# Expert weights in half-megabyte units: 48 units and 24 slots per pair of experts in place of 24 and 12

## The reference, cut to what matters

```python
aff = jax.nn.softmax((h @ w_router).astype(jnp.float32), axis=-1)
gates, idx = lax.top_k(aff.transpose(0, 2, 1), cap)          # cap = 64
xe = h[bidx, idx]
hg = jnp.einsum('becd,edf->becf', xe, w_gate)
hu = jnp.einsum('becd,edf->becf', xe, w_up)
y = jnp.einsum('becf,efd->becd', jax.nn.silu(hg) * hu, w_down)
y = y * gates[..., None].astype(y.dtype)
return jnp.zeros_like(h).at[bidx, idx].add(y)
```

## Time and profile before

| | |
|---|---|
| median of 3 runs | 2509.53 us (2507.8 to 2515.42) |
| the profiled execution, its own time | 2508.35 us |
| span of the trace, first to last instruction | 2506.8 us |
| TensorE busy, share of the span | 90% |
| granted TensorE clock, mean | 0.947 |
| weights of the expert layer | 192 DMAs of 1024 KB, issued by SyncE |
| rate of the DMA engines in the last slices | 420 GB/s |

### The profile page before, as it was taken

One profiled execution on the slowest core, in us unless ns is written; L12 is line 12 of the kernel. 1 busy time (PEld: TensorE's weight loads), 2 busy tenths in 40 slices (PEclk: granted clock), 3 DMA queues, 4 the chain that ended last, 5 costly groups with the idle time before them and its releaser, 6 DMA issues. The chain is left out here.

```text
span 2506.8 us, 43844 instructions
## 1 busy us (share of the span) xinstructions
PE 2248.1 (90%) x18713; PEld 1174.4 (47%) x18713; DVE 951.9 (38%) x1754; ACT 463.2 (18%) x913; POOL 256.6 (10%) x199
## 2 busy tenths in 40 slices
PE   6989988889998998989899977899979879999998
PEld 3543436653463343764444433667634444444442
DVE  1057784331126767533333541443322241111112
ACT  1020431121002142111212332412010200000000
POOL 0021400200020310020014621400000000000000
PEclk9989989999998999999899988999989989999999
DMA  4135011111215300111102001210123559999997
GB/s 157 67 127 186 9 46 36 41 47 54 92 45 208 112 18 30 37 48 57 60 17 76 26 34 61 57 43 25 36 68 118 228 241 406 420 420 420 421 420 299
DMA packets 64653, 332.99 MB, mean 133 GB/s; under 512 B 7648, under 2 KB 11232, under 8 KB 35680
## 3 DMA queue, kind: packets, MB, share of 16 engines
q1 hardware_dynamic: 64480, 330.46, 34.6%
HBM read 320.21 MB, written 5.77 MB: 130 GB/s over the span
## 5 line engine op out<-in xcount | busy, mean ns | idle before, releaser
L427 PE MATMUL ps<-store,side_ring 128*128 128x512 f32 x784 | 400.1, 634 | 24.8 <-DMA side_ring<-in_w_out 8.9
L2473 PE MATMUL ps<-expert_ring,xe 128*64 128x512 f32 x1024 | 223.3, 593 | 3.8 <-DMA expert_ring<-in_w_expert 2.0
L427 PEld LDWEIGHTS ps<-store,side_ring 128*128 128x128 f32 x784 | 137.3, 196 | 180.3 <-issue 148.0
L340 PE MATMUL ps<-store,side_ring 128*128 128x512 f32 x384 | 169.3, 604 | 1.9 <-DVE store L306 1.9
L2473 PEld LDWEIGHTS ps<-expert_ring,xe 128*64 128x64 f32 x1024 | 73.0, 137 | 150.7 <-issue 148.6
L427 PE MATMUL ps<-store 128*128 128x512 f32 x224 | 116.7, 655 | 24.2 <-DMA store<-in_w_merge 23.7
L340 PEld LDWEIGHTS ps<-store,side_ring 128*128 128x128 f32 x384 | 74.4, 194 | 95.6 <-issue 93.3
L2501 PE MATMUL ps<-expert_ring,store 128*64 128x512 f32 x512 | 113.0, 600 | 1.4 <-DVE store L2558 1.4
L1558 PE MATMUL ps<-store,raw 128*128 128x512 f32 x256 | 110.7, 593 | 1.9 <-DVE store L306 1.9
L2530 ACT ACTIVATE store<-ps 128x1024 f32<-128x1024 f32 x16 | 16.4, 1025 | 418.2 <-PE ps L2473 418.2
L2545 DVE SCALAR_TENSOR_TENSOR x<-ps,mod,x 128x512 f32<-128x512 f32 x64 | 48.1, 751 | 109.1 <-PE ps L2450 104.8
(11 more groups left out here) (430 smaller groups left out, 3892.4 us busy)
## 6 DMA issues: line engine op xcount, KB each, us to landing
expert_ring<-in_w_expert SPq DMA_DIRECT2D x192, 1024.0 KB, 16.9
mixed<-in_w_ada SPq DMA_DIRECT2D x24, 1024.0 KB, 4.9
side_ring<-in_w_attn SPq DMA_DIRECT2D x32, 512.0 KB, 3.7
side_ring<-in_w_rwkv SPq DMA_DIRECT2D x20, 512.0 KB, 4.5
raw<-in_ple_gate SPq DMA_DIRECT2D x16, 512.0 KB, 4.0
store<-in_w_merge SPq DMA_DIRECT2D x14, 512.0 KB, 3.9
side_ring<-in_w_conv SPq DMA_DIRECT2D x12, 512.0 KB, 3.7
chosen<-in_w_o SPq DMA_DIRECT2D x8, 512.0 KB, 5.4
```

The lines of the kernel that those rows point to most:

```text
L340: last = nc.tensor.matmul(ps[:, u, :], ring[:, u, k, :], src[:, k, :], start=(k == 0), stop=(k == kt - 1))
L427: ins = self.nc.tensor.matmul(self.ps[:, self.banks[j % banks], :], self.ring[:, j % self.slots, k, :], self.src[:, k, :], start=(k == 0), ...
L2473: last = nc.tensor.matmul(ps[w, 2 * ep + half, :], xe[:, ep, k, :], ring[:, unit % SLOTS, k2, S * half:S * half + S], start=(k == 0), stop ...
```

## The change

A unit becomes half as large, 128 partitions x 1024 fp32 (512 KB, one row tile of one matrix), and there are twice as many: `UNITS = 48`, `SLOTS = 24`. The ring has the same bytes. In HBM the units of gate and up of the same row tile stand behind one another. PE's loop over four groups of two row tiles becomes a loop over 8 row tiles `k`, each with its own waits for two units, four matmuls and two releases. The order of the matmuls and their operands do not change.

```diff
-PAIRS, UNITS, SLOTS = 8, 24, 12
+PAIRS, UNITS, SLOTS = 8, 48, 24
...
-                        for kp in range(4):
-                            pe.wait_ge(s["x_ready"], 1 if first and kp < 2 else r + 2)
-                            gate, up = 8 * ep + 2 * kp, 8 * ep + 2 * kp + 1
+                        for k in range(KT):
+                            pe.wait_ge(s["x_ready"], 1 if first and k < 4 else r + 2)
+                            gate, up = 16 * ep + 2 * k, 16 * ep + 2 * k + 1
                             arrived(gate)
                             arrived(up)
-                            for k2 in range(2):
-                                k = 2 * kp + k2
-                                for half in range(2):
-                                    for unit, w in ((gate, one), (up, two)):
-                                        last = nc.tensor.matmul(ps[w, 2 * ep + half, :], xe[:, ep, k, :],
-                                                                ring[:, unit % SLOTS, k2, S * half:S * half + S],
-                                                                start=(k == 0), stop=(k == KT - 1))
-                                        if k2 == 1 and half == 1:
-                                            last.then_inc(used[unit % SLOTS], 1)
+                            for half in range(2):
+                                for unit, w in ((gate, one), (up, two)):
+                                    last = nc.tensor.matmul(ps[w, 2 * ep + half, :], xe[:, ep, k, :],
+                                                            ring[:, unit % SLOTS, S * half:S * half + S],
+                                                            start=(k == 0), stop=(k == KT - 1))
+                                    if half == 1:
+                                        last.then_inc(used[unit % SLOTS], 1)
...
-                    for fp in range(4):
-                        units = (16 + 2 * fp, 17 + 2 * fp)
+                    for f in range(KT):
+                        units = (32 + 2 * f, 33 + 2 * f)
                         for unit in units:
                             arrived(unit)
...
-                        last = 8 * ep + 7
+                        last = 16 * ep + 15
                         act.wait_ge(used[last % SLOTS], r * TURNS + last // SLOTS + 1)
...
-        ring, extra = sbi("expert_ring", [P, SLOTS, 2, D]), sbi("weighted_last", [P, D])
-        busy = SLOTS - 4
-        lent = ring[:, busy:SLOTS].rearrange("p u k n -> p (u k n)")
+        ring, extra = sbi("expert_ring", [P, SLOTS, D]), sbi("weighted_last", [P, D])
+        busy = SLOTS - 8
+        lent = ring[:, busy:SLOTS].rearrange("p u n -> p (u n)")
...
-    cut = lambda w: w.reshape(8, 2, 4, 2, P, D).transpose(0, 1, 2, 4, 3, 5)
-    up = np.stack([cut(g["w_gate_2"][0]), cut(g["w_up_2"][0])], axis=3).reshape(8, 16, P, 2, D)
-    down = cut(g["w_down_2"][0]).transpose(0, 2, 1, 3, 4, 5).reshape(8, 8, P, 2, D)
+    cut = lambda w: w.reshape(8, 2, 8, P, D)
+    up = np.stack([cut(g["w_gate_2"][0]), cut(g["w_up_2"][0])], axis=3).reshape(8, 32, P, D)
+    down = cut(g["w_down_2"][0]).transpose(0, 2, 1, 3, 4).reshape(8, 16, P, D)
```

More of the change, by code:

```diff
@@ L2492, in pair @@
                         pe.wait_ge(s["out_ready"], r)
-                    for fp in range(4):
-                        units = (16 + 2 * fp, 17 + 2 * fp)
+                    for f in range(KT):
+                        units = (32 + 2 * f, 33 + 2 * f)
                         for unit in units:
                             arrived(unit)
[L2497 to L2505, removed]
+                        for half in range(2):
+                            for ep, w in ((0, one), (1, two)):
+                                last = nc.tensor.matmul(ps[w, 6 + half, :], act_t[:, ep, f, :],
+                                                        ring[:, units[ep] % SLOTS, S * half:S * half + S],
+                                                        start=(f == 0), stop=(f == KT - 1))
+                                if half == 1:
+                                    last.then_inc(used[units[ep] % SLOTS], 1)
                 pe.wait_ge(h_copied, KT)
```

## The result

The change makes the kernel slower: 2520.06 us median (7 runs, 2515.80 to 2520.77) against 2509.53 us (7 runs), a ratio of 1.0032 with a 95% interval of 1.0022 to 1.0041. Run again on another chip it gave 2519.05 us against 2511.62, ratio 1.0026 (1.0014 to 1.0038). The time lies just outside the range of 2505 to 2519.

The account below looks back on a forecast made before the run. The prediction took TensorE to bound the expert layer until the lead was spent, then the DMA rate. Removing 2.05 us of waits and adding 0.67 us of clears to the 2509.53 us median gave 2508.1 us, range 2505 to 2519.

Parts of the forecast that it names:

- the lead: Expert layer: the first 12 units loaded ahead into the ring, eaten by 1.5 us in every pair.
- spare lead: Expert layer: 3.44 us of lead gained against 2.05 us of waits, so 1.39 us left over.
- (1): Expert ring: groups of 8 release units earlier, so the DMA stream starts sooner; 1.72 us of lead gained.
- (2): Gate/up groups: each half group needs its megabyte later than before; another 1.72 us of lead gained.
- the two stalls: TensorE's only waits for weight DMAs before, 0.79 and 1.26 us in pairs 6 and 7; forecast to go.
- (3): TensorE: 96 more groups with waits and releases cost 0; upper end 3.6 us.
- (4): SyncE: issuing twice the DMAs, at most 0.8 us each, keeps up; cost 0.
- (5): Weight DMAs of 512 KB with 4 KB per partition keep 420 GB/s, cost 0; low end 402.
- rival B: Expert weight DMAs: smaller packets slow the rate to 418.5 to 409.6 GB/s, waits return in pairs 5 to 7; 2513.7 us, chance 0.34.
- (6): Kernel end: twelve more semaphores to clear, exposed, cost 0.67 us.
- C: Expert layer: below 409.6 GB/s DMA engines bound most of it, waits from pair 3 on; 2525 us at 402, chance 0.16.
- my three rows: Earlier trace windows over 512 KB DMAs with 4 KB per partition, reading 420, 413 and 402 GB/s.

Follow-up runs that it names:

- fine 1 MB units: Kernel before, but each 1 MB unit holds one row tile of two matrices side by side, waited for and released per 8 matmuls: ratio 0.9990, again 0.9996.

## Why the prediction was wrong, point by point

**What bounds the kernel** held. TensorE sets the pace until the lead is spent, and then the DMA rate does, nearly one for one. With the measured rate my own sum gives 164 x 0.063 = 10.3 us more for the refills, less 1.4 of spare lead, 8.9 us of waits in place of 2.05, plus 0.7 for the clears: +7.6 us. The two measurements of the change are 6.5 and 8 us by their ratios.

**(1) and (2), earlier release and later need: right in kind, but the release was sized too high.** The first refill is issued at 2029.48, 2.1 us behind the first matmul in place of 3.8:

```profile
2029.48 30.63 SPq L2412 DMA_DIRECT2D expert_ring<-in_w_expert  x30
```

So the 1.7 us of (1) are there at the issue. They aren't all there in the stream, because (1) takes the DMA engines to be full from the first refill on. The first 10 us of the stage at the same run length of 8 KB, in the kernel before and in that with fine 1 MB units (second run), columns as in the earlier trace rows:

```profile
2026.69:2036.69 10.00, 10.00 (x49) 3.45 (x50) 5.23 (x5) 0.00 (x0) 0.00 (x0) 1.00 0.52 193
```

```profile
2029.60:2039.60 10.00, 10.00 (x49) 3.45 (x50) 5.23 (x5) 0.00 (x0) 0.00 (x0) 1.00 0.64 232
```

That is 0.39 MB more, or 0.9 us of lead in place of 1.72. With 420 GB/s kept, the two stalls went altogether in the first run of the fine 1 MB units (first pair 57.9 us) and left 1.3 of their 2.5 us in the second (56.2), where my sum had 1.39 us to spare. So even at 420 GB/s the gain of 2.05 us was not safe.

On the other side, I had not counted that slower DMA engines rest less while the ring is full: in 2070 to 2078 us their share is 0.93 in place of 0.80, 8 x 0.13 = 1.0 us that the lower rate gets back. That brings 8.9 down to 7.9, against 9.3 measured (456.4 - 447.1 to the last down; 7.1 by the rows of the waits). Of the 1.4 us between, the release accounts for 0.8 (1.72 - 0.9); the last 0.6 I can't place.

**(3) More waits on TensorE cost nothing**, right. Groups start at 2150.53 and 2152.25, and the loads keep their 0.43 us across both, as in the earlier trace rows:

```profile
2150.10 0.14 PEld L2471 LDWEIGHTS ps<-expert_ring,xe 128*64 128x64 f32 x2 [0.28 <-issue]
2150.53 0.14 PEld L2471 LDWEIGHTS ps<-expert_ring,xe 128*64 128x64 f32 x2 [0.29 <-issue]
...
2151.82 0.14 PEld L2471 LDWEIGHTS ps<-expert_ring,xe 128*64 128x64 f32 x2 [0.28 <-issue]
2152.25 0.14 PEld L2471 LDWEIGHTS ps<-expert_ring,xe 128*64 128x64 f32 x2 [0.28 <-issue]
```

**(4) Twice the DMAs on SyncE cost nothing**, right in its result: the engines stay full. The 0.8 us that I gave as the most for an issue was too low, as the last section shows.

**(5) The rate: this is the step that failed.** I took 420 GB/s for 512 KB DMAs with 4 KB in a partition from one stretch of 4 us, and gave 0.45 to at least 418.5 GB/s. It is 409.6. The stretch of 1907 to 1911 us was short, and it was the most favourable one. A microsecond earlier the same four DMAs read 406 GB/s, and over five microseconds they read 409:

```profile
1906.00:1910.00 4.00, 4.00 (x10) 1.71 (x9) 1.83 (x2) 0.00 (x0) 0.00 (x0) 1.00 0.99 406
1906.00:1911.00 5.00, 5.00 (x13) 2.22 (x12) 1.92 (x2) 0.00 (x0) 0.00 (x0) 1.00 1.00 409
```

The first fill of the ring in the changed kernel has such a stretch too, and shows what follows it:

```profile
1962.00:1966.00 4.00, 4.00 (x11) 1.84 (x10) 0.75 (x1) 0.50 (x1) 0.00 (x0) 1.00 1.00 385
1966.00:1970.00 4.00, 4.00 (x10) 1.71 (x9) 0.00 (x0) 0.12 (x1) 0.00 (x0) 1.00 1.03 421
1970.00:1980.00 10.00, 10.00 (x25) 4.41 (x24) 1.50 (x2) 1.26 (x2) 0.00 (x0) 1.00 1.03 409
```

In the steady stream of the changed kernel, 2100 to 2300 us, the fifty stretches of 4 us read 404 to 411 GB/s, so 421 is above them all, and it doesn't last. In the kernel before, with its runs of 8 KB, the first fill reads

```profile
1966.00:1970.00 4.00, 4.00 (x10) 1.71 (x9) 0.14 (x1) 0.00 (x0) 0.00 (x0) 1.00 1.01 426
1970.00:1980.00 10.00, 10.00 (x25) 4.41 (x24) 1.36 (x2) 1.26 (x2) 0.00 (x0) 1.00 1.01 421
```

and its fifty steady stretches read 412 to 426. I set one stretch of 4 us of small runs beside 200 us of large ones, and with 421 in one place and 406 in another such a stretch can't tell 409 from 420. One word against it was in the rows: the share of the DMA engines was 1.03 for the short runs and 1.01 for the long ones, the same bytes in more recorded packet time. The reason I gave against rival B, that 420 is a limit on bytes, is refuted by 427 GB/s with runs of 16 KB.

The rule of the Trainium skill that I set inside rival B ("DMA: Bandwidth & Descriptors", section "Why small descriptors are slow") has the form that the runs show, a fixed cost for each packet. Worked out as I did it gives 1.2% between 8 and 4 KB (415.2 GB/s, where I wrote 415.6), where the runs show 2.5% (420 to 409.6), 8 to 10 ns a packet. The same page's rule to batch to 1 MiB names the wrong quantity here: DMAs of 512 KB and of 1 MB with the same runs both move 409 GB/s.

**(6) The clears**, right: 74 of them from 2509.7 to 2513.7 us, 4.0 us in place of the 3.4 of the earlier trace rows.

```profile
L190 SPq EVENT_SEMAPHORE_RANGE_CLEAR  x74: 25/25/29, 2509.7 to 2513.7; - x74
```

**The sum of the expert stage**, +6.4 us, is 6.8 to the last down (456.4 - 449.6), 0.7 less for the last down matmuls and 0.4 more behind them, where the clears are. The 6.8 are 4.6 by the rows of the waits (6.6 in place of 2.0) and 0.22 for each of ten more waits. The last down matmuls took 14.7 us, 0.7 of it for a wait of their own, in place of 15.4. Without that wait they are at 14.0, so the clock hid 1.4 us of what the change costs:

```profile
2483.74 12.24 PE L2497 MATMUL ps<-expert_ring,store 128*64 128x512 f32 x56 [1.41 <-DVE store L2554]
2496.49 1.94 PE L2497 MATMUL ps<-expert_ring,store 128*64 128x512 f32 x8 [0.51 <-DMA expert_ring<-in_w_expert]
```

**The chances.** The result lies at the border that I had named between B and C, 409.6 GB/s, and it has the marks of B: the waits came back in pairs 5 to 7, at a DMA share of 1.03, though in four of the eight groups and 0.62 us long by their rows. The two lower of my three rows, 402 and 413 GB/s, lie around it. I let the 420 outweigh them because TensorE streams there as in the expert layer, but the fill of the ring above goes from 421 to 409 with TensorE busy throughout, so that was no reason.

## What to carry to other kernels

With the DMA queue full, DMAs over all 128 partitions and runs of 2 to 16 KB, the rate here was set by the contiguous run in each partition, at 8 to 10 ns for each further packet, and not by the size or number of the DMAs; finer units for finer waits should put two matrices side by side in one run, and not cut the run. Price a transfer's rate from a long stretch of steady stream; move a short one by a microsecond and see what it reads then. Count what a wait costs from the starts of the groups, not from its row alone. Before taking a stall away, see how much is left behind it: here 2 us of waits stood against a rate that costs 0.16 us for each nanosecond per megabyte.

## What the runs showed of the hardware that was not expected

**A stream of DMAs over 64 partitions moved at half the rate.** Two DMAs of 64 partitions in place of one of 128, the same bytes and the same 8 KB runs, ran at 220 GB/s with the DMA engines recorded as full, against 420. It is the partitions of one DMA that differ; why that halves the rate no run here shows.

**SyncE takes longer over an issue when many DMAs are under way.** In 2300 to 2480 us of the changed kernel the median issue takes 939 ns, where it is 333 ns in the kernel before (5 to 10 DMAs of 1 MB under way), and in the changed one at its best (first and last start in us at the end of the row's numbers):

```profile
L2412 SPq DMA_DIRECT2D expert_ring<-in_w_expert x117: 333/939/2804, 2300.1 to 2449.8; - x117
```

These DMAs land 14.8 to 17.2 us behind their issue, which is 11.5 or more at 1.28 us each. Which limit they meet is not shown. It costs nothing here, since the DMA engines stay full (1.03).

**Much of the spread of this kernel is TensorE's clock in three short places.** The last pair's down matmuls follow a pause in which TensorE waits for ScalarE and VectorE. They took 13.98 us in the kernels with units of 2 MB and with fine ones of 1 MB, 15.41 before the change and 16.81 in the second run of the changed kernel, whose window shows the lower of the two levels (0.52, 1.2 GHz) for the first 6 us:

```profile
2488.00:2494.00 6.00, 5.90 (x16) 1.76 (x18) 0.04 (x1) 0.00 (x0) 0.00 (x0) 0.52 1.02 409
```

The first gathering of tokens took between 8.7 and 10.3 us from one execution to the next, with the clock at 0.57 in a stretch that holds most of it, in this execution of the kernel with fine 1 MB units:

```profile
2020.00:2030.00 10.00, 8.10 (x45) 8.02 (x46) 6.33 (x11) 0.00 (x0) 0.00 (x0) 0.57 0.00 0
```

And the first pair took 56.2 us in five profiled executions and 57.9 in six (all but that of the DMAs over 64 partitions): in the second run of the changed kernel (57.9) the clock is 0.83 in its 2050 to 2060 us, where the first run and the kernel before (56.2) have 1.00.

```profile
2050.00:2060.00 10.00, 10.00 (x40) 3.13 (x38) 0.00 (x0) 0.00 (x0) 0.00 (x0) 0.83 1.02 405
```

The change touches none of the three, and together they are as large as its effect.
